# A first MLP whose output products of three quarters are formed by Strassen's scheme, with x kept in the output's memory meanwhile

## The chip, the cores and the metric

The kernel runs on one core of a Trainium2 chip. The metric is the time of one execution on the device, in microseconds (us). Engines are called as in the profile: PE is TensorE, PEld its weight loads, DVE is VectorE, ACT is ScalarE, POOL is GpSimd, SP is SyncE, whose queue issues the DMAs.

## The reference, cut to what matters

Two transformer blocks run one after the other on 512 tokens of width 1024. The change is in the first block's MLP and in what was done beside it:

```
def _sq_relu_mlp(h, w1, w2):
    return jnp.square(jax.nn.relu(h @ w1)) @ w2
...
y_x = _sq_relu_mlp(_modulate(x, g_pre_mlp[l], sh2, sc2), w_mlp_in[l], w_mlp_out[l])
x = x + gt2 * _rmsnorm(y_x, g_post_mlp[l])
```

`w1` is 1024 x 4096 and `w2` 4096 x 1024, all in float32. The second block's memory attention normalises keys (`k = rmsnorm(kv[:, :, 0], k_norm)`), for four heads and 256 memory rows; these are "the keys' statistics".

## The kernel before

Activations lie feature-major: a tile is 128 features by 512 tokens. Each float32 operand is split into a high part that fits the PE's `F32R` type and a low rest, and a product is three matmuls (high·high, high·low, low·high; `products`, L837 to L839). ACT writes the high parts (`copy`, L1744; `ahead`, L1735), DVE (`rest`, L2636) and POOL (`rest`, L3653; `ahead`, L3648) the low ones.

**The first MLP** goes by quarters of the 32 hidden tiles. Hidden tiles 0 to 3 are plain products. The others come in pairs (n = 0 to 13; 2, 4, 4, 4 in the four quarters) by Strassen's scheme: for two output tiles, four pairs of input tiles and two halves of the tokens there are seven products q = 0 to 6, each of 4 x 3 matmuls of 128x256, 84 in all, where plain products would take 48 of 128x512. The seven weight operands ("pieces") are formed on the fly: `even_columns` (ACT) copies two weight blocks into PSUM, `weight_sums` (DVE) forms four sums, `piece_high` (ACT), `piece_low` (DVE, q = 2 and 4) and `piece_rest` (POOL, q = 0, 1, 3, 5, 6) split them. While PE does pair n, the others prepare the pieces of n + 1 and finish pair n - 1: `first_product`, `product_sums` and `first_sum` join the seven products to two tiles, which are then squared (relu on ACT into `tm[0]`, `tm[1]`; max and multiply on DVE), and split into `bH`, `bL`.

After each quarter's pairs come its output products, plain: 8 output tiles x 8 hidden tiles x 3 matmuls of 128x512, 192 in all. ACT copies the first quarter's results to `y`, DVE adds the later ones. In the first quarter's output stage stand the statistics of the four key heads (`statistic_of_halves` on PE, two matmuls each).

**PSUM.** Every pair uses four banks j = 0 to 3 out of a ring of six: q = 0 and 2 go to j = 0, 1 and 3 to j = 1, 4 to j = 2, 5 and 6 to j = 3 (`SUM_OF`). By the ring, bank j = 2 of a pair is bank 0 of the pair before it, and bank j = 3 is bank 1 of the pair before it. PE waits in `claim` for what frees a bank; for j = 1 of an inner pair this is the low part of the odd tile, which `second_low` writes.

**Order.** Every engine has one written order of its work; nothing is scheduled dynamically. Weights come in chunks of 8 blocks through four buffers `raw`, two chunks for a pair, by SP's queue.

**The second MLP** already does both of its products by the scheme, in gate pairs and down pairs. A gate pair gives one joined tile, so a form of the down product is made in every other pair (`inner_sums`, L3538 to L3543, and `joined_sums`).

## Time and profile before

| | |
|---|---|
| median of three runs | 1303.66 us (1303.6 to 1303.84) |
| the profiled execution, its own time | 1303.2 us |
| its span, first to last instruction | 1301.9 us |
| PE busy | 1290.2 us, 99% |
| DVE, POOL, ACT busy | 883.2 us (68%), 790.9 us (61%), 723.2 us (56%) |
| first MLP, PE's products by stage | plain hidden tiles to 296.03; pairs 0 and 1 to 316.19; output to 360.77; pairs 2 to 5 to 401.08; output to 444.63; pairs 6 to 9 to 484.94; output to 528.49; pairs 10 to 13 to 568.80; output of the fourth quarter behind it |

Stages are read from the starts of PE's matmuls. A matmul's own time overlaps with that of the next, so what counts is the distance between starts.

### The profile page before, as it was taken

Reading aid. Unit: us, or ns where it says so; the run is one execution under the profiler, and the core shown is the slowest. Engines: PE = TensorE matmul, PEld = TensorE weight load, DVE = VectorE, ACT = ScalarE, POOL = GpSimd, SP = SyncE. Lnnn points to the kernel's source line nnn. Section 1 sums busy time; section 2 is a strip of 40 time slices with the busy share of each in tenths; the row PEclk is TensorE's granted clock in tenths of the full one; section 3 lists DMA queues with packets and bytes.
Section 4 is the critical chain, followed back from the end, with each engine's and each line's share of the span. In section 5 each row is a group of like instructions: output and inputs, shape, how many; then the busy total and the mean of one; then the engine's idle time right before and its main releaser. Section 6 shows DMA issues by size and latency. Waiting matters only on the chain.

```text
span 1301.9 us, 21566 instructions
## 1 busy us (share of the span) xinstructions
PE 1290.2 (99%) x8286; PEld 1125.3 (86%) x8286; DVE 883.2 (68%) x1520; ACT 723.2 (56%) x1339; POOL 790.9 (61%) x546
## 2 busy tenths in 40 slices
PE   9999999999999999999999999999999999999998
PEld 6787778879898898998788888776789999999998
DVE  5796694966265472642558574747589977987888
ACT  4532585476463363544655556645477655765664
POOL 3643425977376575665557363643377876887785
DMA  9685245333333233233422122111123332333233
GB/s 378 242 310 210 80 153 194 114 114 108 103 106 105 90 104 122 83 98 107 131 91 93 49 66 65 65 62 37 58 75 112 102 110 98 98 114 114 98 102 111
DMA packets 41831, 152.08 MB, mean 117 GB/s; under 512 B 4352, under 2 KB 5120, under 8 KB 40960
## 3 DMA queue, kind: packets, MB, share of 16 engines
q1 hardware_dynamic: 40848, 147.41, 32.9%
q0 software_dynamic: 448, 2.62, 0.5%
q8 instruction: 66, 1.08, 0.3%
q10 hardware_dynamic: 432, 0.67, 0.1%
q14 instruction: 37, 0.30, 0.1%
HBM read 147.80 MB, written 2.10 MB: 115 GB/s over the span
## 4 chain that ended last, share of the span: by engine, by line
PE 85%; DVE 7%; ACT 4%; POOL 3%; issue 1%; DVEq 0%; ACTq 0%; POOLq 0%
PE bank L837 23%; PE bank L839 23%; PE bank L838 23%; PE bank L1367 2%; POOL wL L3648 2%; PE bank L884 1%; PE bank L886 1%; PE bank L885 1%; PE bank L938 1%; POOL acc L3658 1%; DVE small L2826 1%; PE bank L931 1%; PE bank L898 1%; ACT wH L1735 1%; PE bank L923 1%
## 5 line engine op out<-in xcount | busy, mean ns | idle before, releaser
L3648 POOL TENSOR_TENSOR wL<-raw,wH 128x1024 fp32r<-128x1024 f32 (+1 forms) x115 | 284.9, 2485 | 255.3 <-ACT wH L1735 252.2
L837 PE MATMUL bank<-hH,wH 128*128 128x512 f32 (+1 forms) x544 | 210.4, 387 | 1.7 <-POOL wL L3648 0.6
L839 PE MATMUL bank<-hH,wL 128*128 128x512 f32 (+1 forms) x544 | 200.6, 369 | 0.0
L838 PE MATMUL bank<-hL,wH 128*128 128x512 f32 (+1 forms) x544 | 200.3, 368 | 0.0
L1735 ACT ACTIVATE wH<-raw 128x1024 fp32r<-128x1024 f32 (+1 forms) x115 | 120.6, 1050 | 93.5 <-PE bank L839 67.0
L3653 POOL TENSOR_TENSOR wL<-raw,wH 128x512 fp32r<-128x512 f32 (+1 forms) x96 | 122.6, 1278 | 53.7 <-ACT wH L1744 52.9
L837 PE MATMUL bank<-gH,wH 128*128 128x256 f32 x512 | 145.4, 284 | 0.3 <-POOL gL L3653 0.3
L839 PE MATMUL bank<-gH,wL 128*128 128x256 f32 x512 | 144.9, 283 | 0.0
L838 PE MATMUL bank<-gL,wH 128*128 128x256 f32 x512 | 144.9, 283 | 0.0
L837 PEld LDWEIGHTS bank<-hH,wH 128*128 128x128 f32 x544 | 102.8, 189 | 25.3 <-issue 6.5
L839 PEld LDWEIGHTS bank<-hH,wL 128*128 128x128 f32 x544 | 102.6, 189 | 18.0
L838 PEld LDWEIGHTS bank<-hL,wH 128*128 128x128 f32 x544 | 102.9, 189 | 15.5 <-issue 1.9
L837 PE MATMUL bank<-bH,wH 128*128 128x512 f32 (+1 forms) x272 | 102.7, 378 | 0.0
L838 PE MATMUL bank<-bL,wH 128*128 128x512 f32 (+1 forms) x272 | 102.5, 377 | 0.0
L839 PE MATMUL bank<-bH,wL 128*128 128x512 f32 (+1 forms) x272 | 102.4, 377 | 0.0
L3653 POOL TENSOR_TENSOR wL<-t,wH 128x512 fp32r<-128x512 f32 (+1 forms) x66 | 83.6, 1267 | 26.2 <-ACT wH L1744 25.8
L837 PEld LDWEIGHTS bank<-gH,wH 128*128 128x128 f32 x512 | 98.3, 192 | 0.8 <-POOL gL L3653 0.5
L838 PEld LDWEIGHTS bank<-gL,wH 128*128 128x128 f32 x512 | 98.3, 192 | 0.2 <-issue 0.2
L839 PEld LDWEIGHTS bank<-gH,wL 128*128 128x128 f32 x512 | 98.3, 192 | 0.0
L1744 ACT ACTIVATE wH<-raw 128x512 fp32r<-128x512 f32 (+1 forms) x96 | 59.6, 621 | 49.7 <-PE bank L839 48.7
L2636 DVE TENSOR_TENSOR wL<-bank,wH 128x512 fp32r<-128x512 f32 (+1 forms) x94 | 63.3, 674 | 27.5 <-ACT wH L1744 27.5
L837 PE MATMUL bank<-fH,wH 128*128 128x256 f32 x264 | 75.0, 284 | 0.5 <-POOL fSL L3653 0.5
(511 smaller groups left out, 3638.8 us busy)
## 6 DMA issues: line engine op xcount, KB each, us to landing
raw<-in_wall SPq DMA_DIRECT2D x211, 512.0 KB, 3.3
rows<-in_wall SPq DMA_DIRECT2D x24, 1024.0 KB, 11.2
bra<-in_rpbw SPq DMA_DIRECT2D x8, 360.0 KB, 4.6
xq<-in_xt SPq DMA_DIRECT2D x2, 1024.0 KB, 6.7
xT<-in_xn SPq DMA_DIRECT2D x1, 2048.0 KB, 7.9
out_x<-xT SPq DMA_DIRECT2D x6, 256.0 KB, 2.9
vE<-in_ctxt SPq DMA_DIRECT2D x1, 1024.0 KB, 20.7
icn<-in_invc POOLq DMA_DIRECT2D x1, 1024.0 KB, 8.9
```

Of the source, the lines that this page charges most:

```text
L837: matmul(o, a_h, b_h, start=first, stop=False)
L838: matmul(o, a_h, b_l, start=False, stop=False)
L839: return matmul(o, a_l, b_h, start=False, stop=last)
L884: matmul(o, x_h, w_h, start=n == 0, stop=False)
L885: matmul(o, x_h, w_l, start=False, stop=False)
L886: mm = matmul(o, x_l, w_h, start=False, stop=n == len(ks) - 1)
L1367: mm = matmul(o[:, 64 * c:64 * c + 64], e_[:, 128 * c:128 * c + 128], view(e_[:, :], 128 * c + m, [[2 * m, 64 // m], [1, m]]), start=True, ...
L1735: activation(wH[i % NHL][:, 0:n], raw[r % NRAW][:, 0:n], ACT.Copy).then_inc(s.w_hi, 1)
L1744: activation(dst, src, ACT.Copy).then_inc(sem, 1)
L2636: tt(low, src, high.bitcast(F32), ALU.subtract).then_inc(sem, 1)
L3648: tt(wL[i % NHL][:, 0:n], raw[load(c) % NRAW][:, 0:n], wH[i % NHL][:, 0:n].bitcast(F32), ALU.subtract).then_inc(s.w_lo, 1)
L3653: tt(low, src, high.bitcast(F32), ALU.subtract).then_inc(sem, 1)
```

## The change

1. The output products of quarters 0 to 2 become four "outer" pairs each, by the same scheme: 84 matmuls of 128x256 for two output tiles. The MLP is now one list of 26 pairs (`FIRST_MLP`): inner 0, 1; outer 0 to 3; inner 2 to 5; outer 4 to 7; inner 6 to 9; outer 8 to 11; inner 10 to 13. The fourth quarter's output stays plain.
2. For that, each two squared tiles, numbered c = 0 to 15 (c = p + 2 for inner pair p), become a "form" for c below 12: the even tile's first half and the odd tile are split (`even_high`, `odd_high`, `form_lows`), and four sums of 128x256 of them are formed by DVE (`form_sums`) and split by ACT (`sums_of_form_high`) and POOL (`form_sums_rest`).
3. The first outer pair of a quarter does all seven products over the forms i = 0 to 2 first, and then over i = 3 in the order 0, 5, 6, 1, 2, 3, 4.
4. Relu and square are both ACT's now, in place in PSUM. Only hidden tiles 2 and 3 keep DVE's multiply.
5. The sums lie in the memory of `xT`: x is written to the output tensor by DMA when pair 0's weights have been asked for, and read back before the last pair's weights.
6. The keys' statistics move to the fourth quarter's output stage. The rotary angles move to outer pairs 5, 7, 9 and 10, their sines behind outer 11.
7. Banks: j = 1 of an inner pair is freed by the odd tile's low part, j = 3 by the even tile's; for outer pairs by the add or copy to `y`. Hidden tiles 0 to 3 free their banks by low parts 2, 1, 4 and 3.

The diff, cut to its core (removed loops are seen in the listing above):

```diff
-        group([("w_mlp_out", m) for m in range(2)], out_order(quarter))
-        for m in range(2, 8):
-            tile("w_mlp_out", m, out_order(quarter))
+        if quarter < 3:
+            for j in range(4):
+                for i, odd in ((0, 0), (1, 0), (1, 1), (0, 1)):
+                    tile("w_mlp_out", 2 * j + i, range(8 * quarter + odd, 8 * quarter + 8, 2))
+        else:
+            group([("w_mlp_out", m) for m in range(2)], OUT_ORDER)
+            for m in range(2, 8):
+                tile("w_mlp_out", m, OUT_ORDER)
...
+FIRST_MLP = [pair for quarter in range(4)
+             for pair in [("inner", p) for p in range(max(0, 4 * quarter - 2), 4 * quarter + 2)]
+             + [("outer", 4 * quarter + j) for j in range(4 if quarter < 3 else 0)]]
+INNER = {i: at for at, (kind, i) in enumerate(FIRST_MLP) if kind == "inner"}
+OUTER = {i: at for at, (kind, i) in enumerate(FIRST_MLP) if kind == "outer"}
+G = len(FIRST_MLP)
...
+    yS = [at("yS", 4 * K * i, [128, 1024]) for i in range(4)]
+    ySL = [at("ySL", 4 * K * i, [128, 1024], F32R) for i in range(4)]
+    xl = at("xl", R + 92 * K, [128, 256])
...
+        def result_form(n, i, f):
+            c = outer_of(n) - outer_of(n) % 4 + i
+            high = yH[:, i, 256 * f:256 * f + 256]
+            if f == 0:
+                return high, yA[i][:, :], s.lo, LO.b + 2 * c + 2
+            if f < 3:
+                return high, yB[i][:, f - 1, :], s.lo, LO.b + 2 * c + 1
+            at_ = INNER_SUM[f]
+            t = slice(256 * at_, 256 * at_ + 256)
+            return yH[:, i, 768:1792][:, t], ySL[i][:, t], s.rest_g, REST_G.b + 2 * c + at_ // 2 + 1
...
+        def first_freed(n):
+            p, d = inner_of(n), outer_of(n)
+            freed[BANK["sum", n, 0]] = s.sums, 5 * n + 2
+            freed[BANK["sum", n, 2]] = s.sums, 5 * n + 1
+            if d is not None:
+                sem, value = s.y, Y.half + 2 * d
+            else:
+                sem, value = s.lo, LO.b + 2 * p + 4
+            freed[BANK["sum", n, 1]] = sem, value + 1
+            freed[BANK["sum", n, 3]] = sem, value + 2
+        for n in range(G):
+            claimed = set()
+            for q in range(7):
+                j = SUM_OF[q][0]
+                if j not in claimed:
+                    claim(BANK["sum", n, j])
+                    claimed.add(j)
+                if first_out(n):
+                    product_of(n, q, range(3), q in (0, 1, 4, 5), False)
+                else:
                     product_of(n, q, range(4), True, True).then_inc(s.prod, 1)
-                freed[BANK["sum", n, 0]] = s.sums, 5 * n + 2
-                freed[BANK["sum", n, 1]] = s.lo, LO.b + 4 + n + 1
-                freed[BANK["sum", n, 2]] = s.sums, 5 * n + 1
-                freed[BANK["sum", n, 3]] = s.relu_sq, 4 + 2 * n + 2
...
+            if first_out(n):
+                for q in FIRST_ORDER:
+                    mm = product_of(n, q, (3,), False, q in (2, 3, 4, 6))
+                    if q not in (5, 6):
+                        mm.then_inc(s.prod, 3 if q == 4 else 1)
+            first_freed(n)
...
+        def XB(k):
+            return bH[:, k % 8, :], bL[:, k % 8, :], s.lo, LO.b + (k if k % 2 else k + 2)
...
+        for m in range(6):
+            b = BANK["w_mlp_out", m]
+            if m >= 2:
+                tile("w_mlp_out", m, OUT_ORDER, [(claim(b), XB)])
+            freed[b] = s.y_full, m + 1
+            if 0 < m < 5:
+                statistic_of_halves(f"mk{m - 1}", 256)
...
+        def positive(b, dst, count):
+            activation(dst, b, ACT.Relu).then_inc(s.relu, 1)
+            act.wait_ge(s.relu, count)
+        def odd_squared(b, count):
+            positive(b, b, count)
+            square(b, b, s.relu_sq)
+        def even_squared(b, count, c):
+            positive(b, b, count)
+            if c >= 12:
+                square(b, b, s.relu_sq)
+                return
+            if c:
+                act.wait_ge(s.add_v, ADD_V.b + 4 * c)
+            activation(b[:, 0:256], b[:, 0:256], ACT.Square)
+            square(xl[:, :], b[:, 256:512], s.relu_sq)
...
+        def second_tile(n):
             act.wait_ge(s.sums, 5 * n + 4)
...
-            activation(tm[0][:, :], sum_bank(n, 1), ACT.Relu).then_inc(s.relu, 1)
...
+            odd_squared(sum_bank(n, 1), 4 + 2 * inner_of(n) + 1)
+        def first_tile(n):
             act.wait_ge(s.sums, 5 * n + 5)
...
+            even_squared(sum_bank(n, 3), 4 + 2 * inner_of(n) + 2, inner_of(n) + 2)
...
+        def sums_of_form_high(c, side):
+            t = slice(512 * side, 512 * side + 512)
+            act.wait_ge(s.add_v, ADD_V.b + 4 * c + 3 + side)
+            copy(yH[:, c % 4, 768:1792][:, t], yS[c % 4][:, t], s.full)
+        def first_result(n, count):
+            act.wait_ge(s.post, 16)
+            act.wait_ge(s.sums, 5 * n + 3 + count)
+            m = 2 * outer_of(n) + 2 - count
+            copy(y[:, m, :], sum_bank(n, (1, 3)[count - 1]), s.y)
...
+        odd_squared(bank[BANK["w_mlp_in", 1]], 1)
+        even_squared(bank[BANK["w_mlp_in", 0]], 2, 0)
...
+        positive(bank[BANK["w_mlp_in", 3]], tm[0][:, :], 3)
+        positive(bank[BANK["w_mlp_in", 2]], tm[1][:, :], 4)
         piece_high(0, 5)
...
+        odd_high(0)
+        even_high(0)
         piece_high(0, 6)
         even_columns(1)
...
+        for n in range(G):
+            p = inner_of(n - 1)
+            c = 1 if n == 0 else None if p is None else p + 2
+            first_sums = outer_of(n - 1) is not None and outer_of(n - 1) < 4
+            more = n + 1 < G
+            if p is not None:
+                second_tile(n - 1)
+                odd_high(c)
+            if first_sums:
+                first_result(n - 1, 1)
+            if first_out(n):
+                first_tile(n - 1)
+                even_high(c)
+                sums_of_form_high(c, 0)
+                sums_of_form_high(c, 1)
+                c = None
+            if more:
+                piece_high(n + 1, 0)
+            if first_sums:
+                first_result(n - 1, 2)
+            if n == 0:
+                odd_high(1)
+                even_high(1)
+            elif c is not None:
+                first_tile(n - 1)
+                even_high(c)
+            if more:
+                piece_high(n + 1, 1)
+            first_product(n)
+            if not more:
+                ahead("w_mlp_out", 24, 0, 2)
+                continue
+            piece_high(n + 1, 2)
+            if n == 0:
+                sums_of_form_high(0, 0)
+            elif c is not None and c < 12:
+                sums_of_form_high(c, 0)
+            piece_high(n + 1, 3)
+            if n == 0:
+                sums_of_form_high(0, 1)
+            elif c is not None and c < 12:
+                sums_of_form_high(c, 1)
+            piece_high(n + 1, 4)
+            if n == 0:
+                sums_of_form_high(1, 0)
+            piece_high(n + 1, 5)
+            if n + 2 < G:
+                even_columns(n + 2)
+            if n == 0:
+                sums_of_form_high(1, 1)
+            piece_high(n + 1, 6)
...
+        memory_square(0)
+        for m in range(8):
+            if m not in (1, 7):
+                ahead("w_mlp_out", OUT_ORDER[4 if m == 0 else 0], m)
+            act.wait_ge(s.y_full, m + 1)
...
+            if 0 < m < 5:
+                if m > 1:
+                    act.wait_ge(s.mk_n, m - 1)
+                act.wait_ge(s.sums, 5 * G)
+                root(f"mk{m - 1}", 128, rs[(m - 1) % 2], 256)
+            if 0 < m < 4:
+                memory_square(m)
...
+        def plain_squares():
+            odd, even = bank[BANK["w_mlp_in", 3]], bank[BANK["w_mlp_in", 2]]
+            early, late = slice(0, 256), slice(256, 512)
+            dve.wait_ge(s.relu, 3)
+            stt(out=odd, in0=odd, scalar=0.0, in1=tm[0][:, :], op0=ALU.max, op1=ALU.mult).then_inc(s.mult, 1)
+            dve.wait_ge(s.relu, 4)
+            stt(out=even[:, early], in0=even[:, early], scalar=0.0, in1=tm[1][:, early], op0=ALU.max,
+                op1=ALU.mult).then_inc(s.mult, 1)
...
+        def form_sums(c):
+            x_, y_ = squares_of(c)
+            late = tm[1][:, 256:512] if c == 1 else xl[:, :]
+            s1, s4, s3, s2 = (yS[c % 4][:, 256 * n:256 * n + 256] for n in range(4))
+            dve.wait_ge(s.x_moved, 32)
+            dve.wait_ge(s.hi, HI.b + 2 * c + 2)
+            if c == 1:
+                dve.wait_ge(s.mult, MULT.b + 3)
+            else:
+                dve.wait_ge(s.relu_sq, 2 if c == 0 else 2 * c)
+            if c % 4 == 0 and c:
+                dve.wait_ge(s.prod, outer_done(c // 4 - 1))
+            if c == 0:
+                dve.wait_ge(s.sq, SQ.xt + 8)
+            tt(s1, y_[:, 256:512], late, ALU.add).then_inc(s.add_v, 1)
+            dve.wait_ge(s.add_v, ADD_V.b + 4 * c + 1)
+            tt(s2, s1, x_[:, 0:256], ALU.subtract).then_inc(s.add_v, 1)
+            dve.wait_ge(s.add_v, ADD_V.b + 4 * c + 2)
+            tt(s4, y_[:, 0:256], s2, ALU.subtract).then_inc(s.add_v, 1)
+            tt(s3, x_[:, 0:256], late, ALU.subtract).then_inc(s.add_v, 1)
+        def form_lows(c):
+            x_, y_ = squares_of(c)
+            k = 2 * (c % 4)
+            dve.wait_ge(s.hi, HI.b + 2 * c + 1)
+            if c < 12:
+                rest(yB[c % 4], y_.rearrange("p (t n) -> p t n", t=2),
+                     yH[:, c % 4, 256:768].rearrange("p (t n) -> p t n", t=2), s.lo)
+            else:
+                rest(bL[:, k + 1, :], y_, bH[:, k + 1, :], s.lo)
+            dve.wait_ge(s.hi, HI.b + 2 * c + 2)
+            if c < 12:
+                rest(yA[c % 4][:, :], x_[:, 0:256], yH[:, c % 4, 0:256], s.lo)
+            else:
+                rest(bL[:, k, :], x_, bH[:, k, :], s.lo)
+        def added(n, count):
+            m = 2 * (outer_of(n) % 4) + 2 - count
+            dve.wait_ge(s.sums, 5 * n + 3 + count)
+            dve.wait_ge(s.y, Y.half + 8 * (outer_of(n) // 4))
+            tt(y[:, m, :], y[:, m, :], sum_bank(n, (1, 3)[count - 1]), ALU.add).then_inc(s.y, 1)
...
+        plain_squares()
+        form_sums(0)
+        form_lows(0)
+        for n in range(G):
+            p = inner_of(n - 1)
+            c = 1 if n == 0 else None if p is None else p + 2
+            added_ = outer_of(n - 1) is not None and outer_of(n - 1) >= 4
+            if n:
+                first_sum(n - 1)
+            if added_:
+                added(n - 1, 2)
+            if first_out(n):
+                form_sums(c)
+                form_lows(c)
+                c = None
+            if n + 1 < G:
+                weight_sums(n + 1)
+            if c is not None:
+                if c < 12:
+                    form_sums(c)
+                form_lows(c)
+            if n + 1 < G:
+                piece_low(n + 1, 2)
+            product_sums(n)
+            if n + 1 < G:
+                piece_low(n + 1, 4)
+            if outer_of(n) is not None and outer_of(n) >= 4:
+                added(n, 1)
+            if outer_of(n) in (5, 7, 9, 10):
+                next(turn_)
...
+        for m in range(6):
+            dve.wait_ge(s.product, out_done(max(m, 1)))
+            dve.wait_ge(s.y, Y.half + 24)
+            tt(y[:, m, :], y[:, m, :], bank[BANK["w_mlp_out", m]], ALU.add).then_inc(s.y_full, 1)
+            if m < 4:
+                low_sums(f"mk{m}")
+            if 0 < m < 5:
+                dve.wait_ge(s.root, rooted(f"mk{m - 1}"))
+                dve.wait_ge(s.ones, 5)
+                stt(out=kM[:, m - 1, :], in0=kM[:, m - 1, :], scalar=vc("mem_k"), in1=rs[(m - 1) % 2][:, 0:256],
+                    op0=ALU.mult, op1=ALU.mult).then_inc(s.mk_n, 1)
...
+        def form_sums_rest(c, side):
+            t = slice(512 * side, 512 * side + 512)
+            pool.wait_ge(s.full, FULL.b + 2 * c + side + 1)
+            rest(ySL[c % 4][:, t], yS[c % 4][:, t], yH[:, c % 4, 768:1792][:, t], s.rest_g)
...
+        for n in range(G):
+            p = inner_of(n - 1)
+            c = None if p is None or p >= 10 else p + 2
+            if n == INNER[2]:
                 nc.gpsimd.dma_start(cosT[:, :].bitcast(I32), pos.partition_broadcast(128)).then_inc(s.mem_in, 16)
...
+            if first_out(n):
+                form_sums_rest(c, 0)
+                form_sums_rest(c, 1)
+                c = None
+            if n + 1 == G:
+                ahead("w_mlp_out", 24, 0, 2)
+                continue
+            piece_rest(n + 1, 0)
+            piece_rest(n + 1, 1)
+            if n == 0:
+                form_sums_rest(0, 0)
+            elif c is not None:
+                form_sums_rest(c, 0)
+            piece_rest(n + 1, 3)
+            if n == 0:
+                form_sums_rest(0, 1)
+            elif c is not None:
+                form_sums_rest(c, 1)
+            piece_rest(n + 1, 5)
+            if n == 0:
+                form_sums_rest(1, 0)
+            piece_rest(n + 1, 6)
+            if n == 0:
+                form_sums_rest(1, 1)
...
+            if i == last_inner:
+                sp.wait_ge(s.prod, outer_done(2))
+                sp.wait_ge(s.x_moved, 32)
+                nc.sync.dma_start(xT[:, :, :], out).then_inc(s.x_moved, 16)
             weights_load(i)
+            if i == first_inner:
+                sp.wait_ge(s.post, 16)
+                nc.sync.dma_start(out, xT[:, :, :]).then_inc(s.x_moved, 16)
```

## Rows read from the trace of the kernel before

**Rows 1.** The page: busy time of the engines, share of the span, instructions
```profile
PE 1290.2 (99%) x8286; PEld 1125.3 (86%) x8286; DVE 883.2 (68%) x1520; ACT 723.2 (56%) x1339; POOL 790.9 (61%) x546
```

**Rows 2.** Windows: pairs 2 to 5, then output of the second quarter
```profile
core 0: us, PE busy (x) PEld busy (x) DVE busy (x) ACT busy (x) POOL busy (x), PEclk, DMA share, GB/s
...
360.77:401.08 40.31, 40.31 (x337) 40.30 (x336) 26.86 (x46) 25.81 (x46) 29.51 (x23) 1.00 0.31 99
401.08:444.63 43.55, 43.55 (x194) 36.06 (x193) 20.38 (x28) 11.36 (x15) 21.17 (x11) 1.00 0.33 109
```

**Rows 3.** What PE waited for from 296 to 630 us: total, times, longest
```profile
PE bank L837 <- DVE hL L3167: 0.4, 1, 0.4
```

**Rows 4.** Windows: inner pair 8, and a gate pair of the second MLP
```profile
464.79:474.87 10.08, 10.08 (x87) 10.08 (x86) 8.23 (x14) 6.97 (x13) 7.70 (x7) 1.00 0.33 106
...
1126.23:1136.31 10.08, 10.08 (x86) 10.08 (x85) 9.75 (x19) 7.88 (x16) 8.78 (x8) 1.00 0.33 104
```

**Rows 5.** Timeline of ACT beside pair 8 (starts at 464.79): start, us
```profile
464.74 0.60 ACT L1744 ACTIVATE bank<-raw 128x512 f32<-128x512 f32 x1 [0.56 <-DVE wL L2636]
465.28 0.62 ACT L1744 ACTIVATE wH<-tmp 128x512 fp32r<-128x512 f32 x1
...
466.96 0.58 ACT L2086 ACTIVATE tmp<-bank 128x512 f32<-128x512 f32 x1
467.44 0.59 ACT L1744 ACTIVATE bH<-bank 128x512 fp32r<-128x512 f32 x1
...
469.31 0.38 ACT L1744 ACTIVATE rs<-bank 128x256 f32<-128x256 f32 x1 [0.75 <-PE bank L839]
469.59 0.59 ACT L1744 ACTIVATE wH<-bank 128x512 fp32r<-128x512 f32 x1
```

**Rows 6.** Timeline of DVE beside pair 8
```profile
467.02 0.69 DVE L2965 TENSOR_TENSOR bank<-bank,raw 128x512 f32<-128x512 f32 x1
...
469.66 0.68 DVE L3061 SCALAR_TENSOR_TENSOR tmp<-bank,tmp 128x512 f32<-128x512 f32 x1
470.26 0.68 DVE L2636 TENSOR_TENSOR wL<-bank,wH 128x512 fp32r<-128x512 f32 x1
470.86 0.68 DVE L2636 TENSOR_TENSOR bL<-bank,bH 128x512 fp32r<-128x512 f32 x1
472.19 0.42 DVE L2988 TENSOR_TENSOR acc<-bank,rs 128x256 f32<-128x256 f32 x1 [0.64 <-PE bank L839]
...
474.04 0.68 DVE L2636 TENSOR_TENSOR wL<-bank,wH 128x512 fp32r<-128x512 f32 x1
```

**Rows 7.** Timeline of DVE, second MLP: the four sums of a form
```profile
1131.08 0.42 DVE L3538 TENSOR_TENSOR fS<-bank,tmp 128x256 f32<-128x256 f32 x1
...
1132.33 0.41 DVE L3543 TENSOR_TENSOR fS<-bank,tmp 128x256 f32<-128x256 f32 x1
1132.66 0.68 DVE L2636 TENSOR_TENSOR wL<-bank,wH 128x512 fp32r<-128x512 f32 x1
```

**Rows 8.** Timeline of ACT: an operation that reads the one before it
```profile
249.79 0.66 ACT L1754 ACTIVATE bank<-bank,eps 128x512 f32<-128x512 f32 x1 [1.18 <-PE bank L898]
250.48 0.58 ACT L1756 ACTIVATE bank<-bank 128x512 f32<-128x512 f32 x1
```

**Rows 9.** Timeline of ACT: first relu behind the plain hidden tiles
```profile
296.23 0.60 ACT L2061 ACTIVATE tmp<-bank 128x512 f32<-128x512 f32 x1 [0.90 <-PE bank L839]
```

**Rows 10.** Timelines of POOL and PE: PE resumes after a wait
```profile
1272.50 2.54 POOL L3653 TENSOR_TENSOR fSL<-fS,fH 128x512 fp32r<-128x512 f32 x2 [0.19 <-ACT fH L1744]
...
1275.09 0.39 PE L837 MATMUL bank<-fH,wH 128*128 128x256 f32 x1 [0.26 <-POOL fSL L3653]
1275.32 0.28 PE L838 MATMUL bank<-fSL,wH 128*128 128x256 f32 x1
```

**Rows 11.** Timeline of PE where a first down pair ends
```profile
1055.06 0.28 PE L839 MATMUL bank<-fH,wL 128*128 128x256 f32 x1
...
1055.68 0.28 PE L839 MATMUL bank<-fH,pL 128*128 128x256 f32 x1
```

**Rows 12.** Timeline of DVE: first adds to y in the fourth quarter
```profile
579.91 1.28 DVE L3125 TENSOR_TENSOR y<-y,bank 128x512 f32<-128x512 f32 x2 [5.59 <-PE bank L839]
```

**Rows 13.** The page, DMA issues: KB, us to landing
```profile
xT<-in_xn SPq DMA_DIRECT2D x1, 2048.0 KB, 7.9
```

451 lines of the change are left out of this document (152 added, 299 removed).

## The prediction

> **What bounds the kernel now.** I read the page's busy times first: PE is busy 99% of the span, no other engine over 68% [rows 1]. So time is won by fewer columns through PE, and lost wherever PE waits. Then PE's waits over the first MLP: from 296 to 630 us it waited once on another engine for work, 0.4 us, behind the stretch that is changed [rows 3]. The change therefore finds no stall to remove; what it saves is counted on PE alone, and each wait it makes adds in full. Windows give both stages: four inner pairs, 336 matmuls of 256 columns, take 40.31 us, 0.120 us each and 10.08 a pair; an output stage of 192 matmuls of 512 columns takes 43.55 us [rows 2]. The granted clock is 1.00 in each of them, its upper level.
>
> **What is saved.** Four outer pairs have the same 336 matmuls as four inner ones: 40.31 instead of 43.55, 3.24 us a quarter, 9.7 us for three. The statistics' eight matmuls only move.
>
> **What the pairs now ask of the others.** All numbers below are from a pair's start T on PE; its product q starts at T + 1.44 q, and ACT sees product 3 at T + 4.32 + 0.20 (469.31 against 464.79) [rows 5].
>
> Bank j = 3 of a pair is claimed by q = 5, at T + 7.20, and is bank j = 1 of the pair before. It is freed by the odd tile's low part. Before, that ended at 470.86 + 0.68 = 471.54, T + 6.75: 0.45 us in hand [rows 6]. Now DVE does `form_sums` first, which waits for both high parts, which wait for ACT's relus and squares. So I walk through that chain.
>
> Durations: on ACT a 512 column operation follows the last after about 0.53 (0.48 from PSUM), a 256 one lets the next start after 0.28 [rows 5]. One that needs the result before it starts after that one's duration plus 0.03 (0.66 gave 0.69) [rows 8]. Relu or square in place in PSUM isn't in the trace; by relu to SBUF, 0.58, and the root in place, 0.58, I take 0.62 when something depends on it, 0.41 for 256 columns [rows 5, 8]. On DVE: `weight_sums` 2.65, a 512 low 0.60 to the next and 0.68 to its end, `product_sums` 1.85 [rows 6]; the four sums of a form 1.58 (1131.08 to 1132.66), a 256 low 0.34 [rows 7].
>
> **The loop.** `even_columns` for pair n + 2 overwrites the bank that `piece_low(n + 1, 4)` reads, so it starts when that ends. Call its start e. ACT from there: `even_columns` 0.53, piece 6 0.53, relu and square of the odd tile 1.24, its high 0.53, piece 0 0.53, relu of the even tile 0.62, its squares 0.28 + 0.41, `even_high` 0.38, release 0.03: form_sums starts at e + 5.1. DVE: sums 1.58, odd low 0.60, even low 0.34, `piece_low` 0.60, `product_sums` 1.85, `piece_low` 0.68, and 0.05 back to ACT: 5.7. One turn is 10.8 us, against PE's 10.08; before, DVE stood 0.64 us idle for PE within it [rows 6]. The odd low ends at e + 5.1 + 1.58 + 0.68 = e + 7.36. After an outer pair e is -0.05, as before (464.74) [rows 5].
>
> A wait costs PE 0.07 from the release to its first matmul (0.05 in the one of the trace) and 0.10 for restarting (0.23 between two starts instead of 0.12) [rows 10].
>
> - Second inner pair of quarters 1 and 2: 7.31 + 0.07 - 7.20 + 0.10 = 0.3 us.
> - Third and fourth: the loop is behind, e = 0.39: 0.7 us each.
> - First outer pair: three forms of each product come first, so q = 5 starts at 5 x 1.08 = T + 5.40, while DVE and ACT, without piece 0 between, have the odd low at e + 6.83: 7.22 + 0.07 - 5.40 + 0.10 = 2.0 us. PE's fourth-form products then find their sums ready (POOL ends them near T + 9.4, used from T + 9.6 on).
> - Per quarter 3.7, both 7.4 us.
>
> **The start.** Pair 0 starts at 296.03 (296.23 less 0.20) [rows 9]. ACT: relu, square, relu, half squares, two relus that each wait, piece 5, `odd_high`, `even_high`: ends 301.14. DVE: sums, odd low, even low end at 303.77. q = 4 claims hidden tile 0's bank, due 301.79: 2.15 us. Then DVE's order is `weight_sums` (2.65), sums and lows of form 1: 308.94; pair 1 claims tiles 2 and 3's banks with q = 0 and 1, due 308.26: 0.85 us, so T = 309.1. DVE goes on with `piece_low`, `product_sums(0)`, `piece_low`: 312.00. Only then may ACT do `even_columns(2)`, a sums copy, piece 6 (1.6) and the chain of the squares (4.0): 317.63; sums and odd low: 319.92. q = 5 was due at 316.31: 3.8 us, the largest. The first outer pair behind it, with e = 0.40: 2.0 us. Together 8.8 us.
>
> **The rest.** Behind a first outer pair the next one's piece 0 is split late. The second MLP's first down pair shows it: 0.62 for three starts instead of 0.36, 0.26 us [rows 11]; three of them, 0.8. In the fourth quarter, `low_sums(mk0)` stands on DVE behind the first add to y, which waits for the same products that PE has just ended, and PE's statistic waits for it: 0.20 + 0.60 (1.28 for two adds is one after 0.60 [rows 12]) + 0.42 + 0.17 = 1.4 us. Later statistics have a tile's 5.4 us of cover. ACT's four roots and squares there, 1.7 us a tile, lie under the same cover.
>
> Costed at nothing: the two moves of x, 2 MB each. The read of 2 MB took 7.9 us [rows 13]; the write has from the ask for pair 0's weights, some 25 us ahead of the first form sum, and the read is asked for near the start of inner pair 10 and needed 90 us later. The weights queued behind it land some 12 us later and are used 20 us after the ask; without that cover PE would wait up to 8 us. POOL's 7 operations of 1.25 to 1.30 are 9 us a pair, under 10.08. The fourth quarter's inner pairs have no form sums and their odd low comes at T + 4.2, so they run as before. The sines (about 4 us) stand behind an outer pair, where ACT has 4 us and more free. The add to y in outer pairs comes after `piece_low`, due 5 us later.
>
> Is the order "high parts, then sums" only written so, that a measurement might undo it? The rows can't say; DVE and ACT never stand on one bank together there. The Trainium skill, PSUM — Partial Sum Buffer, section "PSUM bank collisions raise a hardware error", says that two engines must not access one bank's partitions at once, reads included. By it the 0.4 to 0.9 us of copies ahead of the sums can't be taken out; without it the sum below would be some 3 us lower.
>
> **Sum.** 8.8 + 7.4 + 0.8 + 1.4 = 18.4 lost, 9.7 saved: +8.7. The profiled execution's 1303.2 becomes 1311.9; it is 0.46 below the median, so 1312.4.
>
> Bounds. If dependent operations in place followed after only 0.48, the pipelined spacing [rows 5], the loop is 10.3 and its odd low at e + 6.9: the waits are 1.3 a quarter and 6.8 at the start, in all 11.6 with the rest: +1.9, 1305.6. If each costs 0.08 more, the loop is 11.1: 4.9 twice, 9.9, 0.8 and 1.6, 22.1 in all: +12.4, 1316.
>
> **Rivals.** *All hidden.* A gate pair of the second MLP has 9.75 us of DVE work in 10.08, form sums in it, and PE loses nothing [rows 4]; if the first MLP bears it as well, 1303.7 - 9.7 = 1294.0. Against: there a form is made in every second pair, and its odd tile is out of the banks earlier. It decides if the waits sum to under 9.7, so more than half of my 18.4 must be absent; up to 1301 I count it here. Chance 0.16.
> *A draw.* The start and the first outer pairs wait as worked out (6.8 and 3 with 1.3 to 2.0), the loop doesn't: 10 to 13 us against 9.7, 1301 to 1305.6. Chance 0.13.
> *The clock.* No stretch read shows it under 1.00 [rows 2, 4], but none has PE waiting 3.8 us. If the 3.8 us wait lets the granted clock fall from 2.4 to 1.2 GHz, a matmul of 256 columns takes 0.24 for 0.12; for half a pair to a whole one that is 5 to 10 us more: 1317 to 1322. The Trainium skill, TensorE: Matmul & The Clock Gate, section "Why this matters for your kernels", warns of such gaps; no row here shows the fall. Chance 0.07.
> The scheme itself is sure to be done: PE's matmuls rise by 3 x 144.
>
> **How the numbers follow.** The worked-out case has 0.64, its own range 1305.6 to 1316. The range 1300 to 1317 leaves out nearly all of the first rival and most of the clock: 0.2. A measurement tells 0.2%, 2.6 us, from no change. Faster (below 1301.1): 0.16 + 0.02. Same (to 1306.3): most of the draw, and a little of the main case, 0.09. Slower: 0.73.
>
> **What would show it.** After the change, PE's waits in this stretch should read: DVE lows (L2636's successor) on a q = 4 matmul of pair 0, on q = 5 of inner pairs and of each first outer pair, 2 us there and near 3.8 in pair 1; inner pairs of quarters 1 and 2 at 10.4 to 10.8 us, outer ones at 10.08, those of the fourth quarter at 10.08; `even_columns` idle until DVE's low each time. If pair 1 shows no gap, or first outer pairs take 10.1 us, my reading of the banks is wrong and the time is near 1294. If the in-place relu and square are far from 0.58, the loop's share moves by four times the difference.

## The result, and the profile after

The changed kernel takes 1315.35 us (median of 4 runs, 1314.12 to 1316.03), where the kernel before takes 1303.75 (median of 4, the three runs of the section above among them). The ratio is 1.0085, 95% interval 1.0073 to 1.0098: slower, by 11.6 us. The profiled execution took 1315.59 us, with a span of 1314.3.

The page of the changed kernel, busy time by engine, answers to [rows 1]. PE is busy 2.1 us less for 432 matmuls more, and the span is 12.4 us longer, so PE now stands still where it did not. All other engines gained work, and none is busy for more than 73% of the span.

```profile
PE 1288.1 (98%) x8718; PEld 1142.2 (87%) x8718; DVE 960.7 (73%) x1685; ACT 782.6 (60%) x1488; POOL 824.3 (63%) x592
```

What PE waited for from 296 to 640 us in the changed kernel (total, times, longest) answers to [rows 3], where the only row is 0.4 us. L2746 is the helper that all low parts go through. Two rows are cut here, of 0.4 and 0.3 us: both waits stand behind the first MLP.

```profile
PE bank L875 <- DVE yB L2746: 10.4, 9, 2.8
PE bank L875 <- DVE yA L2746: 1.9, 1, 1.9
PE bank L945 <- DVE sumL L2746: 1.2, 1, 1.2
...
```

Nine waits for an odd tile's low part (yB), one for an even tile's (yA, pair 0) and the statistic's: the three kinds that the prediction names. Their sum, 13.5 us, is not the whole loss. The windows of PE in the changed kernel show the rest. The second to fourth outer pair of quarter 1 come first, then pieces of the start.

```profile
core 0: us, PE busy (x), PEclk, DMA share, GB/s
421.70:451.95 30.25, 30.25 (x253) 1.00 0.38 122
...
307.00:310.00 3.00, 3.00 (x18) 0.59 0.25 101
310.00:320.00 10.00, 7.81 (x66) 0.99 0.23 68
320.00:327.00 7.00, 6.35 (x31) 0.53 0.20 70
```

Three outer pairs take 30.25 us, 10.08 each: the saving, 9.7 us for three quarters, is there in full. But in two pieces of the start the granted clock is 0.59 and 0.53, so for most of them it was at the lower of its two levels (1.2 GHz, where 1.00 is 2.4). The timeline of PE shows both falls: behind a wait of 1.95 us in pair 0, and behind one of 2.84 us in pair 1, matmuls of 256 columns start 0.21 us apart instead of 0.12.

```profile
304.56 0.39 PE L875 MATMUL bank<-sH,wH 128*128 128x256 f32 x1 [1.95 <-DVE yA L2746]
...
306.32 0.42 PE L876 MATMUL bank<-hL,wH 128*128 128x256 f32 x1
306.53 0.41 PE L877 MATMUL bank<-hH,wL 128*128 128x256 f32 x1
...
320.65 0.58 PE L875 MATMUL bank<-hH,wH 128*128 128x256 f32 x1 [2.84 <-DVE yB L2746]
321.03 0.42 PE L876 MATMUL bank<-hL,wH 128*128 128x256 f32 x1
321.25 0.41 PE L877 MATMUL bank<-hH,wL 128*128 128x256 f32 x1
```

Some 16 matmuls ran so after the first wait (1.4 us lost) and some 26 after the second (2.4 us). The ledger from the starts of PE's matmuls, each gap less the usual spacing, beside the forecast. The restart is counted in: the second start behind a wait comes 0.22 us after the first instead of 0.12.

| place | forecast, us | measured, us |
|---|---|---|
| pair 0, q = 4 | 2.15 | 2.2 |
| slow matmuls behind it | not in the sum | 1.4 |
| start of pair 1 | 0.85 | 0 (PE came late itself) |
| pair 1, q = 5 | 3.8 | 3.3 |
| slow matmuls behind it | not in the sum | 2.4 |
| first outer pair of quarter 0 | 2.0 | 1.0 |
| quarter 1: inner pairs 2, 3, 4, first outer | 0.3, 0.7, 0.7, 2.0 | 0.2, 0.7, 0.7, 2.0 |
| quarter 2: the same | 0.3, 0.7, 0.7, 2.0 | 2.0, 0.7, 0.7, 2.0 |
| first piece behind three first outer pairs | 0.8 | 0.6 |
| statistic | 1.4 | 1.45 |
| sum | 18.4 | 21.3 |

21.3 less 9.7 is 11.6. By the traces, PE needs 324.5 us from pair 0 (296.70) to the first sum of squares behind the fourth quarter (621.23); before, 313.0 (296.03 to 609.03). The difference is 11.5, and 0.7 of the other 0.9 us of the span arises before pair 0, in code that the change leaves alone: the kernels of the experiments below, which share this code, start pair 0 anywhere from 295.93 to 296.94.

### The profile page after: what moved, and what is told of

Its sections match the earlier page's. It is cut to its first block, busy times and chain, and to the rows that moved or that the text cites. A ratio compares the mean times of both kernels' runs of the same rounds, so it can differ in the third digit from the quotient of the medians.

```text
span 1314.3 us, 22875 instructions
## 1 busy us (share of the span) xinstructions
PE 1288.1 (98%) x8718; PEld 1142.2 (87%) x8718; DVE 960.7 (73%) x1685; ACT 782.6 (60%) x1488; POOL 824.3 (63%) x592
## 3 DMA queue, kind: packets, MB, share of 16 engines
q8 instruction: 69, 1.13, 0.4%
## 4 chain that ended last, share of the span: by engine, by line
PE 74%; DVE 12%; ACT 8%; POOL 3%; issue 2%; DMA 1%; DVEq 0%; SPq 0%; ACTq 0%; POOLq 0%
PE bank L875 20%; PE bank L877 20%; PE bank L876 20%; PE bank L1429 2%; POOL wL L3789 2%; PE bank L922 1%; PE bank L924 1%; PE bank L923 1%; PE bank L976 1%; POOL acc L3799 1%; DVE small L2936 1%; ACT bank L2119 1%; ACT yH L1806 1%; DVE wL L2746 1%; PE bank L969 1%
## 5 line engine op out<-in xcount | busy, mean ns | idle before, releaser
L3789 POOL TENSOR_TENSOR wL<-raw,wH 128x1024 fp32r<-128x1024 f32 (+1 forms) x91 | 227.8, 2508 | 227.8 <-ACT wH L1797 224.7
L3794 POOL TENSOR_TENSOR wL<-raw,wH 128x512 fp32r<-128x512 f32 (+1 forms) x120 | 154.0, 1284 | 45.8 <-ACT wH L1806 45.2
L1797 ACT ACTIVATE wH<-raw 128x1024 fp32r<-128x1024 f32 (+1 forms) x91 | 95.1, 1048 | 54.6 <-PE bank L877 28.2
L2746 DVE TENSOR_TENSOR wL<-bank,wH 128x512 fp32r<-128x512 f32 (+1 forms) x118 | 79.6, 675 | 32.5 <-ACT wH L1806 32.5
L1806 ACT ACTIVATE wH<-raw 128x512 fp32r<-128x512 f32 (+1 forms) x120 | 74.6, 622 | 38.4 <-PE bank L877 37.2
L1806 ACT ACTIVATE wH<-bank 128x512 fp32r<-128x512 f32 (+1 forms) x118 | 69.2, 586 | 38.6 <-DVE bank L3081 21.5
L3794 POOL TENSOR_TENSOR pL<-raw,pH 128x512 fp32r<-128x512 f32 (+1 forms) x60 | 77.8, 1297 | 20.4 <-ACT pH L1806 20.4
L875 PE MATMUL bank<-yH,wH 128*128 128x256 f32 x288 | 81.8, 284 | 4.1 <-DVE yB L2746 4.1
L3794 POOL TENSOR_TENSOR wL<-tmp,wH 128x512 fp32r<-128x512 f32 x52 | 67.5, 1298 | 28.3 <-ACT wH L1806 28.1
```

Of the source, the lines that this page charges most:

```text
L875: matmul(o, a_h, b_h, start=first, stop=False)
L1797: activation(wH[i % NHL][:, 0:n], raw[r % NRAW][:, 0:n], ACT.Copy).then_inc(s.w_hi, 1)
L1806: activation(dst, src, ACT.Copy).then_inc(sem, 1)
L2746: tt(low, src, high.bitcast(F32), ALU.subtract).then_inc(sem, 1)
L3789: tt(wL[i % NHL][:, 0:n], raw[load(c) % NRAW][:, 0:n], wH[i % NHL][:, 0:n].bitcast(F32), ALU.subtract).then_inc(s.w_lo, 1)
L3794: tt(low, src, high.bitcast(F32), ALU.subtract).then_inc(sem, 1)
```

## Experiments

Each is run beside the kernel before on the same chip; that one's median was 1303.8 to 1304.1 in these runs. The changed kernel was not run again beside them, so differences from its 1315.35 us are good to about 0.4 us. "Stage" is the time from pair 0 to the same first sum of squares, in the profiled execution.

**1. Another bank for the fourth product.** A pair's fourth bank is the third of the pair before (free early) and no longer its second, which holds the odd tile's squares.

```
+    banks_, fresh = [7, 6, 4, 0], [5, 1]
     for p in range(G):
         for j in range(4):
-            of["sum", p, j] = order[n % 6]
-            n += 1
+            of["sum", p, j] = banks_[j]
+        banks_, fresh = [*fresh, banks_[0], banks_[2]], [banks_[1], banks_[3]]
...
```

> Only the ring of banks is changed: bank 3 of a pair is bank 2 of the pair before it instead of bank 1. My theory (PE waits for the odd tile's low part because of the ring, and the loop of ScalarE and VectorE is longer than a pair): the 0.7 us waits inside pairs and the 2.0 us waits in first outer pairs on q = 5 go, and part of them comes back where the forms themselves are needed, on the even tile's low part in a first outer pair's second pass, 1.5 to 2 us each; in all 7 to 11 us less than the changed kernel's 1315.4, so 1304 to 1308. Rival (the loss is spread: more work beside PE slows every operation, or PE's clock falls whatever waits there are): no gap moves, within 2 us of 1315.4.

Measured: 1311.08 us (1309.6 to 1311.2), ratio 1.0052 (1.0035 to 1.0069). The gain is 4.3 us, where 7 to 11 was expected. The waits of PE in this kernel:

```profile
PE bank L876 <- DVE yA L2747: 9.5, 5, 2.8
...
PE bank L876 <- DVE yB L2747: 0.9, 2, 0.6
...
```

The claims at q = 5 are gone, and PE waits for yA, the last form's even part, as data of each first outer pair: 2.8 us in quarters 0 and 2, 1.4 in quarter 1. So the bank was only where the delay showed. Taking the bank away lets PE run up to the next point at which the same chain of ScalarE and VectorE is due. That chain itself is no shorter. Its turn can be read off the starts of `even_columns` on ACT, one for each pair. In the changed kernel they are 10.75 us apart in quarter 1 (forecast: 10.8; PE's pair is 10.08):

```profile
388.49 0.60 ACT L1806 ACTIVATE bank<-raw 128x512 f32<-128x512 f32 x1 [1.05 <-DVE wL L2746]
...
399.24 0.60 ACT L1806 ACTIVATE bank<-raw 128x512 f32<-128x512 f32 x1 [1.04 <-DVE wL L2746]
```

With the other banks they are 10.75 apart as well (386.06 and 396.81), though PE no longer waits in those pairs.

**2. The odd tile's low part ahead of the form's sums.** The bank is then free after the third of the four sums.

```
+            if p is not None and p < 10:
+                freed[BANK["sum", n, 1]] = s.add_v, ADD_V.b + 4 * (p + 2) + 3
...
             if first_out(n):
+                odd_low(c)
                 form_sums(c)
-                form_lows(c)
+                form_lows(c, False)
...
+                if 2 <= c < 12:
+                    odd_low(c)
```

> VectorE writes the odd tile's low part before it waits for the even tile, in time in which it stood idle, and bank 1 is freed by the third form sum. My theory: the loop loses 0.6 us (10.8 to 10.2), so inner pairs no longer wait, first outer pairs wait 1.0 instead of 2.0 us, pair 1 about 1 us less: 7 to 9 us less than the changed kernel, 1306 to 1308.5. Rival (VectorE's amount of work is what counts, 73% busy): nothing is removed, so no change from 1315.4.

Measured: 1307.05 us (1306.66 to 1307.65), ratio 1.0023 (1.0013 to 1.0033): 8.3 us regained, as expected. The waits of PE:

```profile
PE bank L875 <- DVE yS L3193: 5.1, 4, 2.6
PE bank L875 <- DVE yA L2748: 2.5, 2, 1.9
...
```

All waits of the third and fourth inner pairs are gone. Two things changed at once: the bank is free about 1 us earlier, at the third sum, and the turn is shorter, because the odd low part now fills VectorE's time while ScalarE still works on the even tile. `even_columns` on ACT, at the same place of quarter 1, shows a turn of 10.17 us (the expectation said 10.2):

```profile
385.36 0.60 ACT L1808 ACTIVATE bank<-raw 128x512 f32<-128x512 f32 x1 [0.64 <-DVE wL L2748]
...
395.53 0.60 ACT L1808 ACTIVATE bank<-raw 128x512 f32<-128x512 f32 x1 [0.72 <-DVE wL L2748]
```

Experiment 6, which has this order on the banks of experiment 1, shows what the turn alone is worth.

**3. The statistic's low part ahead of the first add to y.**

```
+        low_sums("mk0")
         for m in range(6):
             ...
-            if m < 4:
+            if 0 < m < 4:
                 low_sums(f"mk{m}")
```

> One edit of the changed kernel: VectorE computes the fourth quarter's first key statistic's low part ahead of the first add to y instead of behind it. My theory: the wait of 1.2 us on sumL (1.47 us of lost matmul starts) goes and nothing takes its place, 1.4 to 1.5 us less than the changed kernel: 1313.9 us beside its 1315.35. Rival: the output banks that the add frees are then late, or another operand of the statistic is, and the gain is under 0.5 us.

Measured: 1313.09 us (1312.73 to 1314.16), ratio 1.0071 (1.0058 to 1.0083): 2.3 us less than the changed kernel. The wait on sumL is gone from the trace and nothing stands in its place: 1.45 of the 2.3 us. Most of the rest is not the edit's: this execution starts pair 0 at 295.93 instead of 296.70, and its stage is 322.8 us instead of 324.5. The clock fell twice here too. It fell once at the start instead of twice (0.96 from 296 to 338 us, 0.88 in the changed kernel), and once in quarter 2's second inner pair, behind a wait of 1.79 us. The timeline of PE:

```profile
469.50 0.48 PE L875 MATMUL bank<-hH,wH 128*128 128x256 f32 x1 [1.79 <-DVE yB L2746]
469.77 0.41 PE L876 MATMUL bank<-hL,wH 128*128 128x256 f32 x1
469.99 0.41 PE L877 MATMUL bank<-hH,wL 128*128 128x256 f32 x1
```

From 469 to 473 us the granted clock is 0.58 here. In the changed kernel, where the same wait is 1.78 us, it is 1.00.

**4. The angles' second part one pair earlier.** These are three operations of VectorE ahead of quarter 2's second inner pair.

```
-            if outer_of(n) in (5, 7, 9, 10):
+            if outer_of(n) in (5, 6, 9, 10):
```

> The second part of the rotary angles moves from outer pair 7 to outer pair 6, work unchanged. The trace after the change shows 2.0 us on q = 5 of the second inner pair of the third quarter, where I had forecast 0.3. My theory: the angles and an add stood on VectorE ahead of that pair's work and made the loop late by 1.5 us: that wait falls to 0.3 to 0.6 us, 1.4 to 1.7 us less, about 1313.8. Rival (the wait comes from the loop itself): same as the changed kernel, within 0.5 us.

Measured: 1312.64 us (1312.18 to 1312.89), ratio 1.0067 (1.0052 to 1.0082): 2.7 us less. The 2.0 us lost in quarter 2's second inner pair are down to 0.2, as in quarter 1, so 1.8 us is the edit's, a little over the 1.4 to 1.7 expected. The stage is 2.7 us shorter; its other 0.9 us is the start, which loses 9.4 us with one clock fall instead of 10.3 with two. The start of this execution is the cleanest test of the prediction's first part, since nothing ran slowly before pair 1. The timeline of PE:

```profile
303.85 0.39 PE L875 MATMUL bank<-sH,wH 128*128 128x256 f32 x1 [1.94 <-DVE yA L2746]
...
309.00 0.39 PE L875 MATMUL bank<-hH,pH 128*128 128x256 f32 x1 [0.58 <-DVE yA L2746]
...
319.95 0.58 PE L875 MATMUL bank<-hH,wH 128*128 128x256 f32 x1 [3.49 <-DVE yB L2746]
...
330.91 0.39 PE L875 MATMUL bank<-yH,wH 128*128 128x256 f32 x1 [0.96 <-DVE yB L2746]
```

Pair 1 starts at 309.00 (forecast: 309.1) and loses 0.84 us with the restart (0.85); its q = 5 comes at 319.95 and loses 3.9 (3.8). Then 14 starts are 0.21 us apart once more, behind the 3.49 us wait; the 1.94 us wait ahead of it brought none.

**5. The suspected cost doubled.** In the forms from the third to the twelfth, the odd low part is computed twice, the first time into unused memory.

```
             dve.wait_ge(s.hi, HI.b + 2 * c + 1)
+            if 2 <= c < 12:
+                tt(tm[0][:, :], y_, yH[:, c % 4, 256:768].bitcast(F32), ALU.subtract)
```

> One edit of the changed kernel: in every form from the third to the twelfth, VectorE computes the odd tile's low part twice (the first time into unused memory), 0.60 us more between the form's sums and the low part that frees the bank. My theory, a turn of ScalarE and VectorE that is longer than TensorE's pair: all ten places where TensorE waits for this bank (one in pair 1, three in each of quarters 1 and 2, three first outer pairs) grow by 0.6 us, 5.5 to 6 us in all: 1321 us. Rival, the waits are single events of the start and VectorE has cover in the loop, where it stands idle for 0.5 to 1 us a pair: 1.5 us or less, 1316 to 1317.

Measured: 1322.51 us (1320.06 to 1323.49), ratio 1.0144 (1.0129 to 1.016), 7.2 us above the changed kernel. The waits of PE:

```profile
PE bank L875 <- DVE yB L2746: 16.4, 10, 3.5
...
```

10.4 us became 16.4. Against the changed kernel's trace each of the ten gaps (restart left out) grew by 0.6: in pair 1 from 3.00 to 3.61, in the first outer pair of quarter 0 from 0.88 to 1.46, in quarter 1 from 0.10, 0.59, 0.59 and 1.87 to 0.70, 1.18, 1.18 and 2.45, in quarter 2 from 1.94, 0.59, 0.60 and 1.87 to 2.55, 1.19, 1.19 and 2.47. `even_columns` starts 11.36 us after the one before it in quarter 1 (388.80 and 400.16), 0.6 more than in the changed kernel. So VectorE's operations between the high parts and the bank's release are on the path at every one of these places, and its idle time elsewhere in the pair covers nothing. Single events of the start would have given 1316 to 1317, by the rival. The 7.2 us between the medians are more than the ten gaps' 6.0. The profiled execution was the fastest of the four; its stage is 4.9 us longer than the changed kernel's, 6.0 for the gaps less about 1 for fewer slow matmuls (some 16 each behind waits of 1.94 and 3.45 us). The other three took 1.7 to 3.4 us more than it, and no trace shows in what.

**6. Both edits, banks and low part.**

> Both earlier edits together: a pair's last bank is the third of the pair before and not its second, and the odd tile's low part stands ahead of the form's sums. The second alone gave 1307.05 us. My theory: the waits for q = 5 go everywhere (2.8 us in pair 1, 0.9 and 1.4 in the first outer pairs), and what is left is the data of the last form, due at T + 7.56 of a first outer pair and 2 to 3 us late in quarter 0, about 0.3 in quarter 1 and 1 to 2 in quarter 2, where the angles stand ahead: 1305.3 us, 1304 to 1306.5. Rival, every wait was one for a bank: about 1300.5 us.

Measured: 1306.18 us (1305.77 to 1306.84), ratio 1.0018 (1.0009 to 1.0027). 0.9 us better than the second edit alone, and as expected what is left is data: 1.9 us in the first outer pair of quarter 0 and 0.9 in quarter 2; besides, pair 0's and pair 1's waits, the statistic, and 0.3 to 0.4 us at a time for GpSimd. Against experiment 1 the low part's order differs, and with it the release of one bank. The median is 4.9 us less. The last form's data, there 2.8, 1.4 and 2.8 us late, are 1.9, 0 and 0.9 us late. These waits are for no bank, so this is the shorter turn by itself. Two waits for a bank at the start of first outer pairs, 0.9 us together, are gone too.

**7. All of it, and another order at the start**, with the squares of tiles 2 and 3 written to scratch memory, so that their banks are free before pair 1. Two pieces of the edit:

```
-            stt(out=odd, in0=odd, scalar=0.0, in1=tm[0][:, :], op0=ALU.max, op1=ALU.mult).then_inc(s.mult, 1)
+            stt(out=tm[0][:, :], in0=odd, scalar=0.0, in1=tm[0][:, :], op0=ALU.max, op1=ALU.mult).then_inc(s.mult, 1)
...
+            if n == 0:
+                form_sums(1)
+                form_lows(1)
```

> The two edits of the version before, the statistic's and the angles' too, and another order at the start: ScalarE makes form 0's high parts as soon as its squares are there, and tiles 2 and 3 come later; VectorE does form 0 first, then the weights' sums, then the squares of tiles 2 and 3, which it writes to scratch memory so that their banks are free before pair 1, and form 1 stands behind the products' sums; pair 0's q = 4 takes tile 1's bank. My theory: pair 0's wait of 2.1 us and pair 1's of 0.7 go, the last form's data in quarter 0 are 2 to 4 us late, quarters 1 and 2 lose under 1 us together and the fourth nothing: 4 to 5 us lost against 9.7 saved, 1299 us (1297.5 to 1302), below the kernel before. Rival: the start's work on VectorE, ScalarE and GpSimd is itself too much for two pairs, and the waits only move: 1303 us or more.

Measured: 1303.81 us (1303.44 to 1304.69), ratio 1.0000 (0.9991 to 1.0009), 5 us above my expectation and where the rival put it (1303 us or more). The waits of pair 0 and pair 1 are gone, the statistic's and the angles' too, but PE waits 3.7 us at the start of the first outer pair. The timeline of VectorE shows why: form 1 there, which now reads scratch memory alone.

```profile
309.28 1.13 DVE L3197 TENSOR_TENSOR yS<-tmp 128x256 f32<-128x256 f32 x1
310.45 1.40 DVE L3199 TENSOR_TENSOR yS<-yS,tmp 128x256 f32<-128x256 f32 x1
311.88 1.40 DVE L3201 TENSOR_TENSOR yS<-tmp,yS 128x256 f32<-128x256 f32 x1
313.21 0.41 DVE L3202 TENSOR_TENSOR yS<-tmp 128x256 f32<-128x256 f32 x1
...
314.14 1.51 DVE L2754 TENSOR_TENSOR yA<-tmp,yH 128x256 fp32r<-128x256 f32 x1
```

And that of GpSimd beside it:

```profile
310.08 1.49 POOL L3823 TENSOR_TENSOR wL<-raw,wH 128x512 fp32r<-128x512 f32 x1
...
314.03 2.78 POOL L3823 TENSOR_TENSOR ySL<-yS,yH 128x512 fp32r<-128x512 f32 x2 [1.03 <-ACT yH L1811]
```

The same operation takes 1.13 to 1.51 us while GpSimd runs and 0.41 where GpSimd stands still (313.00 to 314.03): some 4 us more in one form. The Trainium skill, SBUF — State Buffer, section "Who interferes with whom", says that a VectorE instruction with two inputs in SBUF contends with a GpSimd instruction that reads SBUF, and calls the ports that they share an exclusive lock. The trace agrees: VectorE's operations at 310.45 and 311.88 end 0.28 us after GpSimd's at 310.08 and 311.53 do. By that rule the form should cost 0.42 for each sum again with one input in PSUM. Experiment 8 tests that against the rival.

**8. Squares of tiles 2 and 3 by ScalarE in their own banks**, form 1 straight behind the weights' sums.

```
-        positive(bank[BANK["w_mlp_in", 3]], tm[0][:, :], 3)
-        positive(bank[BANK["w_mlp_in", 2]], tm[1][:, :], 4)
...
+        odd_squared(bank[BANK["w_mlp_in", 3]], 3)
+        odd_high(1)
...
-                odd_high(1)
+                even_squared(bank[BANK["w_mlp_in", 2]], 4, 1)
                 even_high(1)
```

> As the version before it, but tiles 2 and 3 are squared by ScalarE in their own banks, and VectorE makes form 1 from there straight behind the weights' sums, before pair 1. In the version before, VectorE's operations with both inputs in scratch memory took 1.13 to 1.51 us for 256 columns while GpSimd ran, and 0.41 in the one stretch in which GpSimd stood still: about 4 us lost. My theory: with one input from PSUM they take 0.41 again; no claim of pair 1 waits; what is left in quarter 0 is the last form's data, 2 to 3 us late, and 1 to 1.5 us for GpSimd's lows: 1299.5 us (1298.5 to 1301), below the kernel before. Rival: the start is bound by the number of VectorE's operations, wherever they read, and the time stays at 1303 us or more.

Measured: 1300.43 us (1300.15 to 1301.32), ratio 0.9976 (0.9967 to 0.9985). Form 1 in the timeline of VectorE:

```profile
305.97 0.42 DVE L3174 TENSOR_TENSOR yS<-bank,xl 128x256 f32<-128x256 f32 x1
306.43 0.42 DVE L3176 TENSOR_TENSOR yS<-yS,bank 128x256 f32<-128x256 f32 x1
306.88 0.42 DVE L3178 TENSOR_TENSOR yS<-bank,yS 128x256 f32<-128x256 f32 x1
...
307.55 0.41 DVE L2747 TENSOR_TENSOR yA<-bank,yH 128x256 fp32r<-128x256 f32 x1
```

And GpSimd beside it:

```profile
306.53 1.29 POOL L3795 TENSOR_TENSOR wL<-raw,wH 128x512 fp32r<-128x512 f32 x1 [0.82 <-ACT wH L1811]
```

The sums' 0.42 is back while GpSimd runs, as expected. This edit also takes 1.3 us of squares off VectorE, so the two causes aren't told apart by the time alone; the durations show the contention.

**9. In addition, the last form of quarter 0 earlier.**

```
             product_sums(n)
+            if n == 1:
+                first_sum(1)
             if n + 1 < G:
                 piece_low(n + 1, 4)
...
```

> As the version with tiles 2 and 3 squared by ScalarE; behind pair 1, VectorE does the sum that completes its last tile before the low part of the next piece, and ScalarE the last form's high parts before the copy of pair 3's even columns. My theory: the last form of quarter 0 comes 0.9 us earlier, 0.5 to 1 us less than the version before it: 1298.7 us. Rival: pair 3's weight sums are late instead, and the two are the same within 0.3 us.

Measured: 1299.23 us (1299.09 to 1299.81), ratio 0.9966 (0.9954 to 0.9979): 4.6 us below the kernel before, 16 below the changed one, and 1.2 below experiment 8, where 0.5 to 1 was expected. The waits of PE from 296 to 640 us:

```profile
PE bank L876 <- POOL pL L3799: 1.1, 3, 0.4
PE bank L876 <- DVE yS L3180: 0.6, 2, 0.4
PE bank L876 <- POOL ySL L3799: 0.5, 2, 0.3
...
```

The matmuls are those of the changed kernel. Its stage is 308.3 us (296.65 to 604.97), 4.7 below that of before, so 5.0 of the 9.7 us are still lost. The most of it that the waits name is GpSimd's: the next pair's first piece is made late behind each first outer pair, 0.5 us three times. In the profiled executions of experiments 8 and 9 the clock never fell in this stage; their longest waits are 1.6 and 0.4 us.

## Why the prediction was right

Its direction and its reasons held. It said 1312.4 us, with 1305.6 to 1316 for the worked-out case and 1300 to 1317 as the whole range; the time is 1315.35. That the time lies within the worked-out case's own range is in part luck: the ledger has 3.8 us that this case did not count at all, the clock's, and two further misses of about 2 us that nearly cancel.

- **The saving.** 9.7 us forecast; outer pairs take 10.08 us each, as read off inner ones.
- **The loop.** Forecast from `even_columns` at e: the sums at e + 5.1, the odd low part's end at e + 7.36. In quarter 2's second inner pair of the changed kernel e is 463.91, the sums start at 468.94 (e + 5.03) and the low part ends at 470.52 + 0.68 (e + 7.29):

```profile
463.91 0.60 ACT L1806 ACTIVATE bank<-raw 128x512 f32<-128x512 f32 x1 [1.73 <-DVE wL L2746]
...
464.97 0.58 ACT L2119 ACTIVATE bank<-bank 128x512 f32<-128x512 f32 x1
465.58 0.58 ACT L1821 ACTIVATE bank<-bank 128x512 f32<-128x512 f32 x1
```

```profile
468.94 0.42 DVE L3187 TENSOR_TENSOR yS<-bank,xl 128x256 f32<-128x256 f32 x1 [1.58 <-ACT yH L1806]
...
470.52 0.68 DVE L2746 TENSOR_TENSOR yB<-bank,yH 128x512 fp32r<-128x512 f32 x1
```

  The square in place follows its relu after 0.61 us, where 0.62 was taken from [rows 8]. That is why the bounds of this term, 0.48 and 0.70, weren't needed. The turn itself measures 10.75 us, forecast 10.8. Experiment 5 shows it on the path: 0.6 us more on VectorE made each wait 0.6 us longer.
- **Quarters 1 and 2.** Third, fourth and first outer pair to 0.1 us in both. The failed term is quarter 2's second inner pair, 2.0 instead of 0.3. The prediction moved the angles with no cost of their own and gave that pair the same e of -0.05 as in quarter 1. The timeline of VectorE in the changed kernel has three of their operations in 4.36 us, and GpSimd's beside them 1.74 instead of 1.30:

```profile
452.41 4.36 DVE L3138 SCALAR_TENSOR_TENSOR tmp<-tmp 128x512 f32<-128x512 f32 x3
```

```profile
454.47 1.74 POOL L3794 TENSOR_TENSOR pL<-raw,pH 128x512 fp32r<-128x512 f32 x1
456.18 1.75 POOL L3794 TENSOR_TENSOR wL<-raw,wH 128x512 fp32r<-128x512 f32 x1
```

  They take 1.45 us each for 512 columns, both inputs in SBUF, against 0.69 for one with an input in PSUM, which looks like the contention of experiment 7. The one inner pair between them and the wait wasn't enough to make it up. Experiment 4 moved them one pair earlier, and the wait went. There the three took 3.11 us instead of 4.36, so their place and their length changed together, and how much of the wait was the contention's is not shown.
- **The start.** 8.8 us forecast, and 2.2, 0.84, 3.9 and 1.2 us in experiment 4's trace, in all 8.1. The first outer pair was the term that was too high (2.0 against 1.2); 14 slow matmuls behind pair 1's wait make PE itself 1.3 us late there, which would explain it, but no run had the one without the other.
- **The clock.** A rival with 0.07 in the prediction, put down as something that takes the place of the worked-out case. In fact it comes on top of it: 3.8 us in the changed kernel's profile, behind waits of 1.95 and 2.84 us. Its size was below the forecast 5 to 10 us: a fall lasted 12 to 26 matmuls in these traces, not the 42 to 84 of half a pair to a whole one. This is the mis-sized term that matters most: 11.6 less 8.7 is 2.9, the clock gives +3.8, the angles +1.7, the start's waits -2.3 (6.5 against 8.8), the rest -0.3. Where PE ran slowly it comes late to the next claim and finds the bank free (pair 1's start), so part of one loss replaces the other.
- **The statistic.** 1.4 forecast, 1.45 found, and gone in experiment 3.
- **Costed at nothing:** the moves of x took 8.5 and 9.2 us from issue to landing and no wait in the trace names them. PE waited for GpSimd nowhere in the changed kernel's stage, but does in experiments 1 and 6 to 9, up to 0.4 us at a time.

The order "high parts, then sums" on one bank, for which the prediction weighed the rule on two engines in one bank, was not tried, so no run here bears on that rule. A reordering that keeps to it (experiment 2) gave 8.3 us, more than the some 3 us that the prediction put on those copies.

## What to carry to other kernels

Here a scheme that saves columns on a PE at 99% paid in full (9.7 us), but handed its extra sums to a turn of two other engines; compute such a turn from the operation that starts it to the release of what PE claims next, because busy shares of 60% and 73% don't show it. When a wait sits on a buffer, ask whether another buffer removes the delay or only its first symptom: here the bank alone gave 4.3 us of an expected 7 to 11, and the order that shortens the turn and frees the bank sooner 8.3. On VectorE keep one input in PSUM where you can while GpSimd works beside it.
